# Unit vectors of the delta rule by whole tiles, and the paged attention's steps in other lanes

## The chip, the core and the metric

One core of one Trainium2 chip runs the whole program. The time is the device time of one execution in microseconds (us); less is better. The core has five engines with an instruction queue each: TensorE (PE) multiplies matrices into PSUM, VectorE (DVE) and ScalarE (ACT) work on vectors, GpSimd (POOL) on vectors too, and SyncE (SP) only starts transfers. GpSimd starts transfers as well. The engines run beside each other and meet only in semaphores: a waiting instruction holds everything behind it on its own engine.

## The reference

One decoder layer in float32 for a prompt of 512 tokens and a sample group of 8 sequences with 4 new tokens each, so T = 544 token columns in all. A mixer runs four head groups beside each other (block-sparse attention, Mamba-2 SSD, HGRN2, gated DeltaNet), then follow cross-attention and a SwiGLU network. Two parts matter here. The first is the unit vectors that the gated delta rule needs of its queries and keys, per token and head of 64 numbers:

```python
def l2_norm(x, eps=1e-6):
    return x * lax.rsqrt(jnp.sum(x * x, axis=-1, keepdims=True) + eps)
```

The query is also scaled by 1/8, and the kernel forms beta times k and beta times v beside it. The second is the sample group's attention over a paged cache of 16 pages per sequence: scores of all keys, the three best blocks of 256 tokens, a softmax, and the weighted sum of the values:

```python
    k_past = k_cache[layer, page_table].reshape(db, past, H, dh)
    gate = jnp.einsum('bqhd,bnhd->bhqn', q, kmean)
    _, idx = lax.top_k(gate, n_sel)
    p = jax.nn.softmax(sc.astype(jnp.float32), axis=-1)
```

## The kernel before

Activations lie with 128 features on the partitions and the 544 tokens in the free dimension, in two halves of 272 columns (`HT`), since a PSUM bank holds 512 floats. The program is a row of stages; each engine's part of a stage is a generator or function of its own, and a stage ends with a semaphore. The change lies in the stage called `ssm`. There four pieces of work are threaded by hand through each other on TensorE, VectorE and ScalarE alike. The string `LANES` holds one letter for each step: `m` is the main piece (`mixer_lane`), `p` the paged attention of the sample group (`moba_sample_*`), `u` the unit vectors of the delta rule (`unit_*`) and `n` a norm (`ssm_norm_*`). All three engines walk the same string and do their share of each step, so a step that must wait holds the steps behind it on that engine, whatever they belong to.

The main piece has 41 steps: the first is m0. m0 to m18 are the SSD scan over four prompt tiles and the sample tile (m16 is its sample tile, m17 its new sample states, m18 the gating). m19 to m26 are the eight levels of the HGRN2 attention on the prompt and m27 to m29 its three levels on the sample. In a level VectorE forms differences, ScalarE takes their exponential, VectorE multiplies queries and keys and then selects what TensorE has computed (L2309). m30 to m40 are the HGRN2 tail: m30 turns the first tile, and then each of the five tiles has two steps. m40 is the sample's second, and the last of the stage.

The paged attention has 111 steps. The first prepares the queries. Then j0 to j65 turn (transpose) the keys and score them: step j turns half a quarter and scores half j-2. A quarter is four pages, four transfers of 128 KB. Four idle steps follow, in the last of which VectorE ranks the blocks and ScalarE takes nine exponentials (L1553, L1554). T0 to T3 and one more step (called T4 here) turn the probabilities. Then come V0 to V31, one step for each quarter of the values, then a step in which VectorE normalizes, a step in which TensorE picks the heads apart (`pick`), and a last copy. There are four buffers for quarters. Quarter n is loaded by SP if n is even and by GpSimd if n is odd (`load_pages`), four pages each with a page number read from a table ahead of it. Value quarters of V4 and later wait until V(k-4) has been used.

The unit piece has 17 steps (`unit_tensor`, `unit_scalar`, `unit_vector`): ScalarE squares, TensorE sums the squares of each head onto 4 rows with `headsel` (64 ones per head), ScalarE takes Ln and Exp(-0.5 x) of the 4 rows, TensorE spreads each row over the 64 partitions of its head with `pairsel`, and VectorE multiplies out of PSUM, half by half. Six spreads are done: for two tiles of queries, two of keys, and two of beta. All of this uses the banks 5 and 6 and starts once the probabilities have been turned.

The list below writes the groups of steps between two main steps, where G k is what stands ahead of main step k.

```
G       before                                  after
0       queries, j0                             queries, j0
1-14    4, 3, 4, 3 ... of j (j1-49)             4 of j each (j1-56)
15, 16  j50-53; j54-56                          j57-59; j60-62
17, 18  j57-60; j61-63                          j63-65; idle
19, 20  j64 j65 idle; idle idle n               idle; idle n
21, 22  idle T0 n; T1 T2 n                      idle n; n
23, 24  T3 T4; V0 V1 u                          T0 T1; T2 T3
25      V2 V3 u                                 T4 V0
26-29   V4 V5 u; V6 V7 u; V8 V9 u; V10 V11 u    V1-3; V4-6; V7-9; V10-12
30      V12 V13 u                               V13-15
31-34   2 V and 2 u each (V14-21)               3 V and 1 u each (V16-27)
35, 36  V22 V23 2u; V24 V25                     V28 V29 u; V30 V31 u
37-39   V26 V27; V28 V29; V30 V31               u; u; u
40, 41  normalize, pick; copy                   normalize, pick; copy
```

Of the kernel before, what the change touches and what calls it, by code (L numbers as in the profile page):

```python
# [19 lines left out]
ALU = mybir.AluOpType  # L20
# [12 lines left out]
H = 4  # L33
# [34 lines left out]
def build(nc, a, o):  # L68
# [12 lines left out]
    with ctx:  # L81
# [298 lines left out]
        g_A = carve(PROJ, base + 2176, 2176)  # L380
        g_N = carve(PROJ, base + 2 * 2176, 2176)
        g_QK = carve(PROJ, base + 3 * 2176, 2176)
        g_sq = carve(XN, 2 * DH, 2, T)
        g_kb = carve(XN, 2 * DH, 2, T)
        g_norm = XN[0:H, 1216:1216 + T], SC[0:H, 8528:8528 + T]

        m = Carver(XN, 4 * T)
        t_tok = m(512)
# [995 lines left out]
        def moba_sample_tensor(pe):  # L1384
            def turn(j):

                n, c_ = divmod(j, 2)
                if c_ == 0:
                    pe.wait_ge(*pages_sem(n))
                if j >= 2:  # L1390
                    pe.wait_ge(S("keys_turned_s"), j - 1)
                for i in range(4):
                    last = tr(bank(5 + j % 2)[:, i * P:(i + 1) * P], pages[:, n % NPG, i, c_ * P:(c_ + 1) * P], P)
                last.then_inc(S("satt_turned"), 1)

            def score(j):

                n, c_ = divmod(j, 2)
                pg, e = divmod(n, 2)
                pe.wait_ge(S("keys_turned_s"), j + 1)  # L1400
                if j % 16 == 0:
                    pe.wait_ge(S("ms_scores_out"), j // 16 + 1)
                for g_ in range(4):
                    last = mm(bank(7)[32 * g_:32 * g_ + 32, pg % 4 * P:(pg % 4 + 1) * P], ms_qp[:, c_, 2 * g_ + e, :],
                              ms_kt[j % 2][:, g_ * P:(g_ + 1) * P], e == 0 and c_ == 0, e == 1 and c_ == 1)
                last.then_inc(S("satt_scored"), 1)

            pe.wait_ge(S("ms_q"), 1)
            for c_ in range(2):
                last = mm(bank(7)[:, 0:NS], ms_q[:, c_, :], ms_kown[:, c_, :], c_ == 0, c_ == 1)  # L1410
            last.then_inc(S("satt_rows"), 1)
            yield
            for j in range(66):
                if j >= 2:
                    score(j - 2)
                if j < 64:
                    turn(j)
                yield
            for _ in range(4):
                yield  # L1420
            pe.wait_ge(S("satt_exp"), 1)
            for i in range(4):
                if i >= 2:
                    pe.wait_ge(S("satt_pt_out"), i - 1)
                for k in range(4):
                    last = tr(bank(5 + i % 2)[:, k * P:(k + 1) * P], ms_s[:, (4 * i + k) * P:(4 * i + k + 1) * P], P)
                last.then_inc(S("satt_pt"), 1)
                yield
            pe.wait_ge(S("satt_pt_out"), 3)
            tr(bank(5)[0:NS, 0:P], ms_own, P).then_inc(S("satt_pt"), 1)  # L1430
            yield
            pe.wait_ge(S("satt_pt_out"), 5)
            for e in range(2):
                mm(bank(7)[:, e * GW:(e + 1) * GW], ms_pown[0:NS, :], ms_vown[0:NS, :], e == 0, False)
            for n in range(32, 64):
                pg, e = divmod(n - 32, 2)
                pe.wait_ge(*pages_sem(n))
                for g_ in range(4):
                    r = slice(32 * g_, 32 * g_ + 32)
                    last = mm(bank(7)[r, e * GW:(e + 1) * GW], st_all[:, pg, r], pages[:, n % NPG, g_, :], False, pg == NPAGE - 1)  # L1440
                last.then_inc(S("ms_values_used"), 1)
                yield
            yield
            pe.wait_ge(S("satt_o"), 1)
            pe.wait_ge(S("g_beta"), 6)
            pick = ident.rearrange("p (g e h t) -> p g e h t", e=2, h=H, t=TS)
            for e in range(2):
                for c_ in range(2):
                    for h2 in range(2):
                        last = mm(bank(5)[h2 * 64:h2 * 64 + 64, c_ * NS:(c_ + 1) * NS].rearrange("p (g e t) -> p g e t", e=2, t=TS)[:, :, e, :],  # L1450
                                  ms_o[:, e, (2 * c_ + h2) * DH:(2 * c_ + h2 + 1) * DH], pick[:, :, e, 2 * c_ + h2, :], True, True)
            last.then_inc(S("satt_pv"), 1)
            yield
            yield
# [196 lines left out]
        def half(ap, j):  # L1651
            return ap[:, j * HT:(j + 1) * HT]

        def spread_norm(pe, n):

            hp, kind = n % 2, n // 2
            src = rows[:, 2, :] if kind == 2 else g_norm[kind]
            for j in range(2):
                last = mm(bank(5 + j)[:, 0:HT], pairsel[0:H, hp, :], half(src, j), True, True)
            last.then_inc(S("rows_spread"), 1)  # L1660

        def unit_tensor(pe):
            yield
            for x in range(2):
                pe.wait_ge(S("satt_pt_out"), 5)
                pe.wait_ge(S("g_sq"), x + 1)
                if x:
                    pe.wait_ge(S("g_root"), 1)
                for hp in range(2):
                    for j in range(2):  # L1670
                        last = mm(bank(5 + j)[0:H, 0:HT], headsel[:, hp, :], half(g_sq[:, hp, :], j), hp == 0, hp == 1)
                last.then_inc(S("g_sum"), 1)
                yield
                yield
            pe.wait_ge(S("g_root"), 3)
            for n in range(6):
                if n:
                    pe.wait_ge(S("g_beta"), n)
                spread_norm(pe, n)
                yield  # L1680
                yield

        def unit_scalar(s):
            def squares(x):
                if x:
                    s.wait_ge(S("g_sum"), x)
                for hp in range(2):
                    last = A.activation(g_sq[:, hp, :], (gq, gk)[x][:, hp, :], ACT.Square)
                last.then_inc(S("g_sq"), 1)

            squares(0)
            yield
            yield
            for x in range(2):
                s.wait_ge(S("g_sum"), x + 1)
                for j in range(2):
                    last = A.activation(half(g_norm[x], j), two(5)[j][0:H, :], ACT.Ln, bias=eps[0:H, :])
                last.then_inc(S("g_root"), 1)
                if x == 0:
                    squares(1)  # L1700
                    yield
                    yield
            s.wait_ge(S("g_root"), 2)
            for x in range(2):
                last = A.activation(g_norm[x], g_norm[x], ACT.Exp, scale=-0.5)
            last.then_inc(S("g_root"), 1)
            yield
            for _ in range(12):
                yield

        def unit_vector(v):
            for _ in range(5):
                yield
            for n in range(6):
                yield
                hp, kind = n % 2, n // 2
                v.wait_ge(S("rows_spread"), 2 + n + 1)
                for j in range(2):
                    if kind == 0:
                        last = V.scalar_tensor_tensor(half(gq[:, hp, :], j), half(gq[:, hp, :], j), SCALE, two(5)[j], ALU.mult, ALU.mult)  # L1720
                    elif kind == 1:
                        last = tt(half(gk[:, hp, :], j), half(gk[:, hp, :], j), two(5)[j], ALU.mult)
                    else:
                        v.wait_ge(S("g_beta"), 4)
                        tt(half(g_kb[:, hp, :], j), half(gk[:, hp, :], j), two(5)[j], ALU.mult)
                        last = tt(half(gv[:, hp, :], j), half(gv[:, hp, :], j), two(5)[j], ALU.mult)
                last.then_inc(S("g_beta"), 1)
                yield


# [725 lines left out]
        def gdn_scalar(s):  # L2456
            hgrn_norm_scalar(s, 0)
            for i, (t0, w, _) in enumerate(TILES):
                s.wait_ge(S("g_m"), i + 1)
                ex = hl(g_p1[:, i % 4, :], w)  # L2460
                A.activation(ex, ex, ACT.Exp).then_inc(S("g_exp"), 1)
                if i < 4:
                    s.wait_ge(S("rows_spread"), 8 + i + 1)
                    A.activation(half(g_logd[:, i // 2, :], i % 2), bank(3 + 4 * (i % 2))[:, 0:HT], ACT.Copy).then_inc(S("rows_spread_out"), 1)
            s.wait_ge(S("rows_spread_out"), 4)
            link(A.activation(g_kbg, g_logd, ACT.Exp), "s")
# [408 lines left out]
        def mixer_lane(eng, ssm, hgrn):  # L2875
# [3 lines left out]
            yield from hgrn  # L2879


        LANES = "m".join(["pp"] + ["pppp", "ppp"] * 9 + ["ppp"] + ["ppn"] * 3 + ["pp"] + ["ppu"] * 7 + ["ppuu"] * 5
                         + ["pp"] * 5 + ["p"])

        def lanes(main, pages_, unit, norm):
            steps = {"m": main, "p": pages_, "u": unit, "n": norm}
# [148 lines left out]
```

## Time and profile before

| | |
|---|---|
| median of three runs | 1516.91 us (1513.17 to 1518.27) |
| the profiled execution's own time | 1517.02 us |
| its span in the trace | 1515.3 us |
| TensorE busy with matmuls | 1358.2 us, 90% |
| VectorE, ScalarE, GpSimd busy | 658.7, 467.9, 442.6 us |
| granted TensorE clock, mean | 0.907 of full speed |
| chain that ended last | TensorE 75%, VectorE 15%, ScalarE 4%, DMA 2% |

The stage runs from about 281 to 555 us of the span. A row of the timeline has the start, the length, the engine, the line, the operation, what it writes and reads, how many, and in brackets the idle time ahead of it with what ended it. L258 is the helper for matmuls, L261 the one for turning, L626 the one for VectorE's two-tensor operations. A float32 matmul or turn stands as two records. `W_scratch` holds the quarters. The clock column is 1.00 at 2.4 GHz and 0.50 at 1.2 GHz.

### The profile page before, as it was taken

The page shows a single profiled execution, that of the slowest core. Times are in us where ns is not written, and L with a number is a line of the kernel's source. Part 1 is how long each engine was busy: PE and PEld are TensorE (multiplying, and loading weights), DVE is VectorE, ACT ScalarE, POOL GpSimd, SP SyncE. Part 2 cuts the span into 40 slices and gives each one's busy share as a digit, 9 for nine tenths or more (in the row PEclk, how much of TensorE's full clock was granted, in tenths as well). Part 3 has the DMA queues.
Part 4 walks back from the last instruction along what each step waited for, and adds up shares of the span by engine and source line. Part 5 has one row for each costly group of instructions (what it writes and reads, how often), then busy time and mean ns, then how long its engine had stood idle before and what let it go on. Part 6 is the DMA issues. An engine that isn't in the chain of part 4 may idle for free.

```text
span 1515.3 us, 24848 instructions
## 1 busy us (share of the span) xinstructions
PE 1358.2 (90%) x10080; PEld 1184.4 (78%) x10080; DVE 658.7 (43%) x1104; ACT 467.9 (31%) x769; POOL 442.6 (29%) x370
## 2 busy tenths in 40 slices
PE   5997999889767976888989898989899999989999
PEld 4997987656554556787879784439899999989998
DVE  4569944254665236653242924310763333330003
ACT  3322244254233014123345423203532222222221
POOL 5424431323103402003525050003234433434330
PEclk8998999879757556998969999999999999999999
DMA  4222230346306630003333040451223223222321
GB/s 122 79 62 70 74 114 1 118 147 192 106 0 196 183 111 1 1 7 119 112 113 98 29 167 22 169 185 56 70 76 93 84 86 96 84 77 77 91 64 60
DMA packets 177556, 136.85 MB, mean 90 GB/s; under 512 B 15011, under 2 KB 165972, under 8 KB 177442
## 3 DMA queue, kind: packets, MB, share of 16 engines
q1 hardware_dynamic: 167906, 113.85, 24.8%
q0 software_dynamic: 7200, 20.23, 4.4%
q8 instruction: 80, 1.31, 0.4%
q10 hardware_dynamic: 2336, 1.18, 0.3%
q14 instruction: 34, 0.28, 0.1%
HBM read 127.27 MB, written 7.96 MB: 89 GB/s over the span
## 4 chain that ended last, share of the span: by engine, by line
PE 75%; DVE 15%; ACT 4%; issue 2%; DMA 2%; POOL 1%; SPq 1%; DVEq 0%; POOLq 0%; ACTq 0%
PE PS L258 69%; PE PS L261 6%; DVE PROJ L1746 2%; DVE SC L626 1%; DVE PROJ L626 1%; DVE XN L887 1%; DVE XT L626 1%; DVE XN L626 1%; POOL W_LO L242 1%; DMA W_scratch<-in_cache_moba_v 1%; DVE PROJ L1747 1%; DVE XN_parts L878 1%; DVE RSQ L885 0%; DVE OM L1595 0%; DMA PROJ<-in_x_sample 0%
## 5 line engine op out<-in xcount | busy, mean ns | idle before, releaser
L242 POOL TENSOR_TENSOR W_LO<-W,W_HI 128x1024 fp32r<-128x1024 f32 (+1 forms) x130 | 317.3, 2445 | 797.8 <-ACT W_HI L233 797.8
L258 PE MATMUL PS<-XN_parts,W_HI 128*128 128x272 f32 x1184 | 341.9, 289 | 0.0
L258 PE MATMUL PS<-OM_parts,W_HI 128*128 128x272 f32 x960 | 279.0, 291 | 0.0
L258 PE MATMUL PS<-SC_parts,W_HI 128*128 128x272 f32 (+2 forms) x832 | 246.7, 296 | 14.7 <-POOL W_LO L242 13.5
L258 PE MATMUL PS<-SC_parts,W_LO 128*128 128x272 f32 (+2 forms) x832 | 243.1, 292 | 0.0
L258 PEld LDWEIGHTS PS<-XN_parts,W_HI 128*128 128x128 f32 x1184 | 224.6, 190 | 0.0
L258 PE MATMUL PS<-OM_parts,W_LO 128*128 128x272 f32 x704 | 203.9, 290 | 0.0
L233 ACT ACTIVATE W_HI<-W 128x1024 fp32r<-128x1024 f32 (+1 forms) x130 | 134.1, 1041 | 207.5 <-PE PS L258 207.5
L258 PEld LDWEIGHTS PS<-OM_parts,W_HI 128*128 128x128 f32 x960 | 183.2, 191 | 0.1
L258 PEld LDWEIGHTS PS<-SC_parts,W_HI 128*128 128x128 f32 x832 | 159.3, 191 | 19.3 <-POOL W_LO L242 12.5
L258 PEld LDWEIGHTS PS<-SC_parts,W_LO 128*128 128x128 f32 x832 | 159.1, 191 | 0.0
L258 PE MATMUL PS<-PROJ_parts,W_HI 128*128 128x272 f32 (+2 forms) x608 | 153.1, 294 | 5.0 <-DVEq L2873 5.0
L258 PEld LDWEIGHTS PS<-OM_parts,W_LO 128*128 128x128 f32 x704 | 132.3, 188 | 0.0
L258 PEld LDWEIGHTS PS<-PROJ_parts,W_HI 128*128 128x128 f32 x608 | 109.1, 193 | 5.4 <-DVEq L2873 5.3
L258 PE MATMUL PS<-PROJ_parts,W_LO 128*128 128x272 f32 (+2 forms) x256 | 75.7, 296 | 0.0
L258 PE MATMUL PS<-SC,XN 64*64 64x4 f32 (+3 forms) x384 | 69.6, 327 | 0.0
L449 POOL DMA_DIRECT2D W_scratch<-in_cache_moba_v x64 | 34.3, 536 | 113.8 <-PE PS L258 83.4
L626 DVE TENSOR_TENSOR SC<-SC 128x272 f32<-128x272 f32 (+6 forms) x68 | 36.8, 544 | 70.5 <-ACT SC L820 50.9
L1147 ACT ACTIVATE PROJ<-PS 128x512 f32<-128x512 f32 (+1 forms) x76 | 44.9, 597 | 65.1 <-PE PS L261 52.8
L261 PE MATMUL PS<-CN,W_scratch 128*128 128x128 f32 x272 | 51.4, 319 | 14.1 <-ACT SC L1554 12.2
L258 PE MATMUL PS<-SC 64*128 64x128 f32 (+7 forms) x404 | 52.7, 345 | 11.7 <-DVE PROJ L626 5.2
L258 PE MATMUL PS<-PROJ,XN 128*128 128x128 f32 (+3 forms) x280 | 43.3, 306 | 20.1 <-DVE XN L626 19.6
(375 smaller groups left out, 2259.6 us busy)
## 6 DMA issues: line engine op xcount, KB each, us to landing
W<-in_w_gu SPq DMA_DIRECT2D x44, 512.0 KB, 3.7
W<-in_w_in SPq DMA_DIRECT2D x30, 512.0 KB, 3.6
W_scratch<-in_cache_moba_k SPq DMA_DIRECT2D x64, 128.0 KB, 2.7
W_scratch<-in_cache_moba_k POOLq DMA_DIRECT2D x64, 128.0 KB, 2.6
W_scratch<-in_cache_moba_v SPq DMA_DIRECT2D x64, 128.0 KB, 2.1
W_scratch<-in_cache_moba_v POOLq DMA_DIRECT2D x64, 128.0 KB, 2.8
W<-in_w_xkv SPq DMA_DIRECT2D x16, 512.0 KB, 3.5
W<-in_w_down SPq DMA_DIRECT2D x16, 512.0 KB, 3.6
```

Source lines behind the costliest of these rows:

```text
L233: nc.scalar.activation(hi_lo(n)[0], raw_chunk(n), ACT.Copy)\
L242: nc.gpsimd.tensor_tensor(hi_lo(n)[1], raw_chunk(n), hi_lo(n)[0].bitcast(F32), ALU.subtract).then_inc(S("weights_split"), 1)
L258: return nc.tensor.matmul(out, lhsT, rhs, start=start, stop=stop, skip_group_check=True)
L261: return nc.tensor.transpose(out, in_, ident[0:k, 0:k])
L449: eng.dma_start(pages[:, n % NPG, i, :], cache[0].rearrange("g p h d -> g p (h d)")[bass.ds(ids[i], 1)].rearrange("g p n -> (g p) n"))\
L626: return V.tensor_tensor(out, x, y, op)
L878: V.scalar_tensor_tensor(lo(k)[:, TOKENS[run][j]], XT[:, k, TOKENS[run][j]], par(GAINS[run][1] + k), hi(k)[:, TOKENS[run][j]].bitcast(F32) ...
L887: last = V.scalar_tensor_tensor(xn[:, k, c_], xn[:, k, c_], par(GAINS[run][0] + k), rsq[:, c_], ALU.mult, ALU.mult)
L1147: return A.activation(o_, i_, ACT.Copy)
L1746: V.scalar_tensor_tensor(dst[:, d:SEQ], src[:, 0:SEQ - d], wt[3 - d], dst[:, d:SEQ], ALU.mult, ALU.add)
L1747: last = V.scalar_tensor_tensor(ds_, win_[:, :, 3 - d:7 - d], wt[3 - d], ds_, ALU.mult, ALU.add)
```

## The change

The unit piece now works on one tile of 128 by 544 at a time, for four tiles (two of queries, two of keys): ScalarE squares the tile, TensorE multiplies the squares by `blk64`, a block matrix of ones, so that each partition gets the sum of its own head, ScalarE takes Ln out of PSUM and Exp(-0.5 x) over the whole tile, and VectorE multiplies from SBUF in one instruction. Only beta is still spread with `pairsel`. The piece has nine steps and three buffers of squares in place of two tiles of squares and two of norm rows. The string `LANES` is written anew, as in the list above. The counts in the waits of other stages follow.

```diff
-        g_sq = carve(XN, 2 * DH, 2, T)
+        g_sqs = [carve(XN, 2 * DH + i * T, T) for i in range(3)]
...
-            pe.wait_ge(S("g_beta"), 6)
+            pe.wait_ge(S("g_beta"), UNITS + 2)
...
         def unit_tensor(pe):
-            yield
-            for x in range(2):
-                pe.wait_ge(S("satt_pt_out"), 5)
-                pe.wait_ge(S("g_sq"), x + 1)
-                if x:
-                    pe.wait_ge(S("g_root"), 1)
-                for hp in range(2):
+            for x in range(UNIT_STEPS):
+                n = x - 1
+                if 0 <= n < UNITS:
+                    if n == 0:
+                        pe.wait_ge(S("satt_pt_out"), 5)
+                    else:
+                        pe.wait_ge(S("g_root"), 2 * n - 1)
+                    pe.wait_ge(S("g_sq"), n + 1)
                     for j in range(2):
-                        last = mm(bank(5 + j)[0:H, 0:HT], headsel[:, hp, :], half(g_sq[:, hp, :], j), hp == 0, hp == 1)
-                last.then_inc(S("g_sum"), 1)
+                        last = mm(bank(5 + j)[:, 0:HT], blk64, half(g_sqs[n % 3], j), True, True)
+                    last.then_inc(S("g_sum"), 1)
+                elif x in (5, 7):
...
+                    for j in range(2):
+                        last = mm(bank(5 + j)[:, 0:HT], pairsel[0:H, x // 7, :], half(rows[:, 2, :], j), True, True)
+                    last.then_inc(S("rows_spread"), 1)
                 yield
+
+        def unit_scalar(s):
+            for x in range(UNIT_STEPS):
+                n = x - 2
+                if 0 <= n < UNITS:
+                    s.wait_ge(S("g_sum"), n + 1)
+                    for j in range(2):
+                        last = A.activation(half(g_sqs[n % 3], j), two(5)[j], ACT.Ln, bias=eps)
+                    last.then_inc(S("g_root"), 1)
+                    s.wait_ge(S("g_root"), 2 * n + 1)
+                    A.activation(g_sqs[n % 3], g_sqs[n % 3], ACT.Exp, scale=-0.5).then_inc(S("g_root"), 1)
+                if x < UNITS:
+                    if x == 3:
+                        s.wait_ge(S("g_beta"), 1)
+                    A.activation(g_sqs[x % 3], unit_of(x), ACT.Square).then_inc(S("g_sq"), 1)
                 yield
...
         def unit_vector(v):
+            for x in range(UNIT_STEPS):
+                n = x - 2
+                if 0 <= n < UNITS:
+                    v.wait_ge(S("g_root"), 2 * n + 2)
+                    V.scalar_tensor_tensor(unit_of(n), unit_of(n), SCALE if n < 2 else 1.0, g_sqs[n % 3], ALU.mult, ALU.mult)\
+                        .then_inc(S("g_beta"), 1)
+                elif x in (6, 8):
+                    hp = x // 8
+                    v.wait_ge(S("rows_spread"), 2 + hp + 1)
+                    v.wait_ge(S("g_beta"), UNITS)
...
-        LANES = "m".join(["pp"] + ["pppp", "ppp"] * 9 + ["ppp"] + ["ppn"] * 3 + ["pp"] + ["ppu"] * 7 + ["ppuu"] * 5
-                         + ["pp"] * 5 + ["p"])
+        LANES = "m".join(["pp"] + ["pppp"] * 14 + ["ppp"] * 3 + ["p", "p", "pn", "pn", "n", "pp", "pp", "pp"] + ["ppp"] * 5
+                         + ["pppu"] * 4 + ["ppu", "ppu"] + ["u"] * 3 + ["pp", "p"])
```

## Rows read from the trace of the kernel before

**Rows 1.** The view by windows: engines' busy time, granted clock (PEclk), three stretches

```profile
core 0: us, PE busy (x) PEld busy (x) DVE busy (x) ACT busy (x) POOL busy (x), PEclk, DMA share, GB/s
460.00:470.00 10.00, 10.00 (x121) 7.13 (x114) 8.13 (x15) 5.56 (x7) 4.29 (x8) 1.00 0.52 170
...
510.00:520.00 10.00, 10.00 (x48) 4.85 (x44) 3.00 (x10) 0.00 (x0) 3.54 (x7) 0.50 0.44 125
...
560.00:580.00 20.00, 19.98 (x104) 16.15 (x102) 8.39 (x18) 6.11 (x10) 0.00 (x0) 0.50 0.25 82
```

**Rows 2.** Timeline of TensorE, key steps and the start of the levels

```profile
306.17 0.66 PE L258 MATMUL PS<-PROJ,W 128*32 128x128 f32 x8 [2.81 <-ACT PROJ L1147]
...
358.54 0.43 PE L258 MATMUL PS<-PROJ,W 128*32 128x128 f32 x8
...
359.49 0.43 PE L258 MATMUL PS<-PROJ,W 128*32 128x128 f32 x8
...
392.36 3.69 PE L258 MATMUL PS<-PROJ,SC 32*128 32x512 f32 x8
...
400.32 2.79 PE L258 MATMUL PS<-PROJ,W 64*128 64x128 f32 x32 [0.32 <-issue]
```

**Rows 3.** Timeline of VectorE: new sample states, ranking, and the first step after levels

```profile
396.17 2.48 DVE L626 TENSOR_TENSOR XN<-XN,PS 128x512 f32<-128x512 f32 x4 [5.42 <-PE PS L258]
...
419.75 0.46 DVE L626 TENSOR_TENSOR SC<-SC 128x64 f32<-128x64 f32 x2
...
481.54 0.35 DVE L2309 COPY_PREDICATED PROJ<-CN,PS 32x64 f32<-32x64 int32 x2 [5.35 <-PE PS L258]
```

**Rows 4.** Timeline of ScalarE: end of the exponentials, a table load, two squares

```profile
426.45 0.18 ACT L1554 ACTIVATION_READ_ACCUMULATOR SC<-SC 128x1 f32 x1
...
428.46 1.28 ACT L1981 ACT_TABLE_LOAD   x1
...
449.96 1.19 ACT L1688 ACTIVATE XN<-PROJ 128x544 f32<-128x544 f32 x2
```

**Rows 5.** Timeline of TensorE: probabilities, levels, and first value steps

```profile
426.69 1.12 PE L261 MATMUL PS<-CN,W_scratch 128*128 128x128 f32 x4 [12.15 <-ACT SC L1554]
...
453.15 1.94 PE L258 MATMUL PS<-W_scratch,PROJ 128*32 128x256 f32 x16
...
462.49 2.82 PE L258 MATMUL PS<-SC 64*128 64x128 f32 x32
```

**Rows 6.** Timeline of GpSimd: issues of the value quarters

```profile
455.77 1.71 POOL L449 DMA_DIRECT2D W_scratch<-in_cache_moba_v  x3 [53.94 <-PE PS L258]
...
471.55 2.30 POOL L449 DMA_DIRECT2D W_scratch<-in_cache_moba_v  x4 [2.27 <-issue]
476.11 2.30 POOL L449 DMA_DIRECT2D W_scratch<-in_cache_moba_v  x4 [2.26 <-issue]
```

**Rows 7.** Timeline of TensorE: value steps, unit steps and tail

```profile
477.12 1.93 PE L258 MATMUL PS<-W_scratch,PROJ 128*32 128x256 f32 x16 [3.61 <-DMA W_scratch<-in_cache_moba_v]
...
489.15 0.69 PE L261 MATMUL PS<-CN,SC 128*128 128x128 f32 x2 [5.66 <-DVE SC L626]
...
492.06 2.18 PE L258 MATMUL PS<-XN,CN 4*128 4x272 f32 x4
...
531.25 0.43 PE L258 MATMUL PS<-SC,XN 64*64 64x128 f32 x2
...
535.16 1.08 PE L258 MATMUL PS<-W_scratch,PROJ 128*32 128x256 f32 x8 [1.15 <-DMA W_scratch<-in_cache_moba_v]
537.64 1.04 PE L258 MATMUL PS<-CN,W 128*64 128x16 f32 x16 [1.40 <-DVE W L1526]
```

**Rows 8.** Timeline of VectorE: a unit step, the masked values of the sample, the stage's end

```profile
499.29 0.79 DVE L626 TENSOR_TENSOR PROJ<-PROJ,PS 128x272 f32<-128x272 f32 x2 [3.56 <-PE PS L258]
...
533.02 2.49 DVE L626 TENSOR_TENSOR SC<-XN,CN 32x512 f32<-32x512 f32 x4
...
550.97 1.23 DVE L626 TENSOR_TENSOR XN<-XN,SM 128x1024 f32<-128x1024 f32 x1 [3.46 <-PE PS L258]
```

More of the change, by code:

```diff
@@ L382, in build @@
         g_QK = carve(PROJ, base + 3 * 2176, 2176)
-        g_sq = carve(XN, 2 * DH, 2, T)
+        g_sqs = [carve(XN, 2 * DH + i * T, T) for i in range(3)]
         g_kb = carve(XN, 2 * DH, 2, T)
-        g_norm = XN[0:H, 1216:1216 + T], SC[0:H, 8528:8528 + T]
         m = Carver(XN, 4 * T)
@@ L1652, in half @@
             return ap[:, j * HT:(j + 1) * HT]
[L1654 to L1660, printed above, removed]
-        def unit_tensor(pe):
-            yield
-            for x in range(2):
-                pe.wait_ge(S("satt_pt_out"), 5)
-                pe.wait_ge(S("g_sq"), x + 1)
-                if x:
-                    pe.wait_ge(S("g_root"), 1)
-                for hp in range(2):
-                    for j in range(2):
-                        last = mm(bank(5 + j)[0:H, 0:HT], headsel[:, hp, :], half(g_sq[:, hp, :], j), hp == 0, hp == 1)
-                last.then_inc(S("g_sum"), 1)
[L1673 to L1680, printed above, removed]
+        UNITS = 4
@@ new lines, in build, with unit_of @@
+        UNIT_STEPS = 9
+        def unit_of(n):
+            return (gq, gk)[n // 2][:, n % 2, :]
+        def unit_tensor(pe):
+            for x in range(UNIT_STEPS):
[6 more added lines that the diff above has]
+                    pe.wait_ge(S("g_sq"), n + 1)
+                    for j in range(2):
+                        last = mm(bank(5 + j)[:, 0:HT], blk64, half(g_sqs[n % 3], j), True, True)
+                    last.then_inc(S("g_sum"), 1)
+                elif x in (5, 7):
+                    if x == 5:
+                        pe.wait_ge(S("g_root"), 2 * UNITS - 1)
+                    else:
+                        pe.wait_ge(S("g_beta"), UNITS + 1)
+                    for j in range(2):
+                        last = mm(bank(5 + j)[:, 0:HT], pairsel[0:H, x // 7, :], half(rows[:, 2, :], j), True, True)
+                    last.then_inc(S("rows_spread"), 1)
@@ L1681, in unit_tensor @@
                 yield
         def unit_scalar(s):
[L1684 to L1708, printed above, removed]
+            for x in range(UNIT_STEPS):
[11 more added lines that the diff above has]
+                    A.activation(g_sqs[x % 3], unit_of(x), ACT.Square).then_inc(S("g_sq"), 1)
@@ L1709, in unit_scalar @@
                 yield
         def unit_vector(v):
[L1712 to L1724, printed above, removed]
+            for x in range(UNIT_STEPS):
[8 more added lines that the diff above has]
+                    v.wait_ge(S("g_beta"), UNITS)
+                    for j in range(2):
@@ L1725, in unit_vector @@
                         tt(half(g_kb[:, hp, :], j), half(gk[:, hp, :], j), two(5)[j], ALU.mult)
                         last = tt(half(gv[:, hp, :], j), half(gv[:, hp, :], j), two(5)[j], ALU.mult)
-                last.then_inc(S("g_beta"), 1)
+                    last.then_inc(S("g_beta"), 1)
                 yield
@@ L2462, in gdn_scalar @@
                 if i < 4:
-                    s.wait_ge(S("rows_spread"), 8 + i + 1)
+                    s.wait_ge(S("rows_spread"), 4 + i + 1)
                     A.activation(half(g_logd[:, i // 2, :], i % 2), bank(3 + 4 * (i % 2))[:, 0:HT], ACT.Copy).then_inc(S("rows_spread_out"), 1)
```

## The prediction

> **What bounds the kernel now.** Read the page first: TensorE is busy for 90% of the span and carries 75% of the chain that ended last, so TensorE's waits and its clock are what can change. The change touches one stage, 281 to 555 us, so the next view is TensorE's timeline there. It shows three regimes.
>
> In the key steps TensorE is nearly always busy. At the upper clock one j step starts 0.95 us after another (358.54, 359.49) [rows 2]; the few gaps follow ScalarE's exponentials of the SSD scan, such as 2.81 us at 306.17 [rows 2], and after that gap the same score step takes 0.66 us in place of 0.43 for a while.
>
> In the eight levels (400 to 470 us) VectorE and ScalarE alternate, and TensorE has time to spare. Its longest wait is 12.15 us ahead of 426.69, for the last exponential of the paged softmax, because T0 stands in front of level 2 in G21 [rows 5]. It looks like the prize of this change, but is not: ScalarE itself does those exponentials until 426.63, and level 2's own exponential stands behind them on ScalarE in both kernels [rows 4].
>
> From 489 to 531.7 us (tail and values) TensorE is busy throughout. Its granted clock is 0.50, that is 1.2 GHz, in 510 to 520 though it is busy for 10.00 of 10 us, while 460 to 470 with the same 10.00 had 1.00 [rows 1]. Beside it runs a second bound: GpSimd issues four transfers of a value quarter in 2.30 us, and then spends 2.26 us on "issue", the page numbers of the next one, so it starts one quarter every 4.56 us (471.55, 476.11) [rows 6]. As it brings every second quarter, the values can't go faster than 2.28 us each. TensorE has met this bound once as a real wait, 3.61 us at 477.12 [rows 7].
>
> **1. Key steps at four a lane.** The number of steps is unchanged, only five more of them stand ahead of m17 (66 against 61). At 0.95 us, less the last two, which only score, that is 4.2 us. Against it, steps moved up fill the gaps behind exponentials: one step more fits ahead of each early exponential, and where the gap shrinks, the slow clock may not follow it. From the 2.81 us gap and its like I take 3 us back; bounds 0 and 8. m17's matmuls (392.36) [rows 2] come 1.2 us later, and so do VectorE's additions at 396.17 that close the sample states [rows 3]. Level 0 can't start before these end. Before, j61 to j65 hid that wait (the row at 400.32 has no wait but 0.32) [rows 2]; now TensorE stands idle for about 2.5 us there. That costs nothing by itself, since VectorE leads the levels, but their start goes 1.2 us later.
>
> **2. Softmax and levels.** VectorE's chain from 396.17 to the ranking at 419.75 [rows 3] has the same instructions in the same order, so it is 1.2 us late. Moving T0 behind m22 takes its copy out of ScalarE's queue: the table load at 428.46 can start at the end of the exponentials, 426.63, so 1.8 us are won [rows 4]. T0 to T4 now stand in G23 to G25, where TensorE has slack. Net: the levels are 0.6 us earlier from G22 on, and their period by VectorE is what it was. The won 12.15 us of TensorE turn into other idle time.
>
> **3. Values start later.** Before, V0 and V1 run at 453.15 (two in 1.94 us, 0.97 each at the low clock) [rows 5], so V1 ends at 455.1, and GpSimd starts the next quarter at 455.77 [rows 6]. Now V1 stands behind level 6 (m25), whose matmuls are at 462.49 and last 2.82 us at the upper clock, twice that at the lower [rows 5]. V1 ends at 465.5 to 469; I take X = 467, 12 us later. What of V2 to V13 ran in the shadow of the levels must now run after them, and the page numbers pace it: V5 can be used at X + 6.3 (issue 0.7 after V1, four transfers in 2.6, then about 3 to land, as 473.85 to 477.12 for V11), and V(5+2k) at X + 6.3 + 4.56 k [rows 6, 7]. V11 is at X + 20. Level 2 of the sample (m29) stands behind V12, so at X + 22; its result and the tail's preparation take VectorE and ScalarE 7.6 us (481.54 to 489.15, less 0.8 for a unit step that stands between) [rows 3, 7]. So m30 turns its first tile at X + 29 to 30, after V15 (X + 29.1 and its own 1): 497 against 489.15, **+7.9 us**.
>
> **4. Tail with values and units.** Before, m30 to m38 take from 489.15 to 531.68, 42.5 us, with 16 value steps and five unit steps of TensorE among them [rows 7]. Now the same main steps hold V16 to V31, 16 again, and six unit steps: four block sums and two spreads. Both are two float32 matmuls of 128 partitions by 272 columns, as the row at 492.06, 2.18 us (its weights are 4 rows high, and the row of a 128-row pair elsewhere is no longer, the columns being the same) [rows 7]. One more is **+2.2 us**. The two dropped head sums stood among the levels, where they were hidden: 0. Page waits: V17, V19 and V21 are due at X + 33.7, 38.2, 42.8 while TensorE, at 2.28 us of pages a value against 0.97 of its own, has only 1.2 to 1.8 us of main work between groups of three. I count 5 us of waits until V21, and none after, when units and main steps cover it: **+5 us**, bounds 2 and 8. The clock: before, this stretch was at the low level but for its last part (the row at 531.25 is 0.43 for two matmuls) [rows 7]; I take the same. Check from the other side: V31 can't land before X + 6.3 + 13 times 4.56 = X + 65.6 = 532.6, and m36, m37, m38 and two spreads still stand behind it, 10 us at the upper clock and 17 at the lower, so m38 ends at 543.6 to 551. The sum above gives 531.7 + 15.1 = 546.8, within that.
>
> **5. Units on ScalarE and VectorE.** ScalarE loads a table for Ln and one for Exp in each of four steps, 1.28 us each, with about four passes of 0.6: some 5 us a step, ten of 20 us in all being table loads [rows 4]. ScalarE does nothing else in the tail. A lane there lasts about 9 us, so neither VectorE, which waits for it, nor the main step queued behind VectorE's wait is late: 0; if a lane were under 6 us, it would cost 1 us each. VectorE's last unit step (four products, twice 0.79) now stands directly ahead of m39, whose masked values (2.49 us) and the normalization lead to `pick`: **+1.5 us** [rows 8].
>
> **6. The end.** From the end of m38 at 531.68 to VectorE's first instruction after m40 at 550.97 are 19.3 us [rows 7, 8]. Ahead of V31 at 535.16, TensorE waited for its page; that about 0.9 us is gone, as V31 is done long before: **-0.9 us**.
>
> The sum is 7.9 + 2.2 + 5 + 1.5 - 0.9 = 15.7 us later at the end of the stage; everything behind it moves along. Against the profiled execution's own 1517.02 us (0.1 above the median) that is 1532.7, and I say 1532.5.
>
> **Rivals.** (a) *TensorE gets the upper clock in the tail.* For it: 531.25 shows that it comes back there [rows 7]. Against it: the page waits leave new gaps, and 510 to 520 was busy without one and stayed low [rows 1]. Then only pages bound the tail: V31 at 532.6, 10 us of TensorE, 19.3 - 0.9 + 1.5 of end, less 5 if m40 too is fast: 557.5 to 562.5, +7 to +11; I say 1526. The Trainium skill's page "TensorE: Matmul & The Clock Gate" (Part 1, The HAM clock gate) says that the gate follows how busy the array has recently been and opens after a short busy stretch; by that rule this rival would be the rule and not the exception. The row of 510 to 520 speaks against it, so it keeps a small chance.
>
> (b) *The low clock holds all through*, also in levels and the end of the tail: X is 469, m38 takes the 17 us. m38 at X + 6.3 + 59.3 + 17 + some 3 of blocked value steps = 554.6, and the end +23 to +26: 1542.
>
> (c) *The key steps win what I hold for lost:* all early gaps and slow stretches close, 8 instead of 3 us. Then X is 462 and all behind it 5 us earlier: 1527.5, with (a) 1520, no change that can be told.
>
> (d) *Faster, by the clock at the stage's end.* If TensorE arrives at m40 at the upper level and keeps it into the next stage, where 560 to 580 are 19.98 us busy at 0.50 [rows 1], up to 10 us are won there and 5 in m40. With (a)'s +7 that already counts m40, the time is 1514 or less. [...]
>
> (e) *The change does nothing:* not open here, since V1 stands behind level 6 by the order of the steps.
>
> **How the numbers follow.** Forecast (1526.5 to 1538) 0.48; (a) 0.13; (b) 0.14; (c) 0.12, a third of it within 0.3% of before; (d) 0.10; something that takes back about all, 0.03. About 0.3%, 4.5 us, is what can be told from no change. Faster: (d) and a tenth of what takes back all, 0.10. Same: the rest of that 0.03, 0.04 of (c) and the low edge of (a), 0.03: 0.10. Slower: 0.80. The range leaves (d) out below and the worst of (b) above: 1517 to 1543.
>
> **What would show it.** After the change, V1 should end at 465 to 469; GpSimd should issue at a strict 4.56 us from there to V15 and past it, and TensorE's waits in G27 to G33 should be put down to pages of the values; the wait of 12.15 us should be gone and the ranking within 3 us of 419.75; m30 at about 497; `pick` waiting some 5 to 7 us for VectorE; the stage's end near 566. It is wrong if the ranking comes more than 5 us earlier, if value steps come faster than one in 2.28 us for long, or if 490 to 550 shows a clock near 1.00.

## The result, and the profile after

| | before | after |
|---|---|---|
| median | 1515.04 us (4 runs, 1512.83 to 1518.27) | 1542.72 us (4 runs, 1541.14 to 1543.84) |
| ratio to before | | 1.018, 95% interval 1.0156 to 1.0204 |
| profiled execution, its span | 1517.02, 1515.3 us | 1541.14, 1539.2 us |
| TensorE busy in the span | 1358.2 us | 1353.8 us |

The change costs 1.8%, 27.7 us between the medians and 24.1 us between the two profiled executions. TensorE does 4.4 us less work and waits for more. The first view is the chain that ended last, from the page of the changed kernel: TensorE has lost share to issue and ScalarE, and the page numbers (L439 on GpSimd's queue) are on it.

```profile
PE 72%; DVE 16%; ACT 5%; issue 4%; DMA 1%; POOLq 1%; POOL 1%; SPq 0%; DVEq 0%; ACTq 0%
PE PS L258 66%; PE PS L261 6%; DVE PROJ L1733 2%; DVE SC L626 1%; DVE PROJ L626 1%; POOLq L439 1%; DVE XN L626 1%; DVE XN L887 1%; DVE XT L626 1%; POOL W_LO L242 1%; DVE PROJ L1734 1%; DVE XN_parts L878 1%; DVE PROJ L2296 1%; DVE RSQ L885 0%; DVE OM L1595 0%
```

TensorE's timeline of the changed kernel, at the steps that answer to [rows 2, 5, 7]: first key page, m16, the two key steps that only score, m17, levels 0, 2 and 3, T0 T1, V0, level 6, V1 to V3, V7 V8, m30, V21, a unit step at the upper clock, two more waits in the tail, the last outputs of m38, and `pick`.

```profile
284.30 1.12 PE L261 MATMUL PS<-CN,W_scratch 128*128 128x128 f32 x4 [2.87 <-DMA W_scratch<-in_cache_moba_k]
...
382.20 6.73 PE L258 MATMUL PS<-SC 32*64 32x32 f32 x72
...
392.06 1.41 PE L258 MATMUL PS<-PROJ,W 128*32 128x128 f32 x16
393.40 7.19 PE L258 MATMUL PS<-PROJ,SC 32*128 32x512 f32 x8
403.33 5.10 PE L258 MATMUL PS<-PROJ,W 64*128 64x128 f32 x32 [2.73 <-DVE XN L626]
...
422.71 5.10 PE L258 MATMUL PS<-SC 64*128 64x128 f32 x32 [2.03 <-DVE PROJ L2296]
437.57 5.10 PE L258 MATMUL PS<-SC 64*128 64x128 f32 x32 [9.76 <-DVE PROJ L2296]
442.60 1.97 PE L261 MATMUL PS<-CN,W_scratch 128*128 128x128 f32 x8
...
460.26 1.08 PE L258 MATMUL PS<-W_scratch,PROJ 128*32 128x256 f32 x8
461.28 5.13 PE L258 MATMUL PS<-SC 64*128 64x128 f32 x32
466.34 1.75 PE L258 MATMUL PS<-W_scratch,PROJ 128*32 128x256 f32 x24
...
478.40 1.94 PE L258 MATMUL PS<-W_scratch,PROJ 128*32 128x256 f32 x16 [1.63 <-DMA W_scratch<-in_cache_moba_v]
...
497.30 0.69 PE L261 MATMUL PS<-CN,SC 128*128 128x128 f32 x2
...
510.03 1.08 PE L258 MATMUL PS<-W_scratch,PROJ 128*32 128x256 f32 x8 [3.51 <-DMA W_scratch<-in_cache_moba_v]
...
516.07 1.18 PE L258 MATMUL PS<-XN,CN 128*128 128x272 f32 x4
...
521.25 1.73 PE L258 MATMUL PS<-W_scratch,PROJ 128*32 128x256 f32 x16 [3.56 <-DMA W_scratch<-in_cache_moba_v]
526.69 1.08 PE L258 MATMUL PS<-W_scratch,PROJ 128*32 128x256 f32 x8 [3.71 <-DMA W_scratch<-in_cache_moba_v]
...
549.34 0.69 PE L258 MATMUL PS<-SC,XN 64*64 64x128 f32 x2
556.82 1.04 PE L258 MATMUL PS<-CN,W 128*64 128x16 f32 x16 [6.79 <-DVE W L1526]
```

The wait of 12.15 us for the softmax [rows 5] is gone, and in its place level 3 waits 9.76 us for VectorE. Two rows of VectorE in the changed kernel mark the ranking and the end of the stage.

```profile
424.28 0.46 DVE L626 TENSOR_TENSOR SC<-SC 128x64 f32<-128x64 f32 x2
...
570.14 1.22 DVE L626 TENSOR_TENSOR XN<-XN,SM 128x1024 f32<-128x1024 f32 x1 [3.46 <-PE PS L258]
```

Where the time came from is read by marks, each counted from the first turned key page (before at 286.37, after at 284.30), since the part ahead of the stage differed by 2 us between the two traces. The ranking is the mark that the row at 424.28 answers to, m38 ends with the last of its outputs (549.34, 0.69 long), and the end of the stage is the row at 570.14. Two rows of the kernel before, its first turned key page and its m16:

```profile
286.37 1.11 PE L261 MATMUL PS<-CN,W_scratch 128*128 128x128 f32 x4 [1.94 <-DMA W_scratch<-in_cache_moba_k]
...
379.81 5.63 PE L258 MATMUL PS<-SC 32*64 32x32 f32 x72
```

| mark | before | after | later by |
|---|---|---|---|
| m17 starts | 106.0 | 109.1 | 3.1 |
| ranking | 133.4 | 140.0 | 6.6 |
| m30 | 202.8 | 213.0 | 10.2 |
| end of m38 | 245.3 | 265.7 | 20.4 |
| end of the stage | 264.6 | 285.8 | 21.2 |

The waits summed by releaser, 440 to 560 us, say which resource: of the changed kernel TensorE waited 11 times for value pages, and GpSimd had 14 gaps that nothing but its own page numbers filled. In the kernel before these were 3 waits of 6.5 us in all and 7 gaps of 12.8.

```profile
POOL W_scratch L449 <- issue: 28.8, 14, 2.8
PE PS L258 <- DMA W_scratch<-in_cache_moba_v: 27.8, 11, 3.7
```

The windows 430 to 490 and 490 to 550, before and after (columns as in [rows 1]):

```profile
430.00:490.00 60.00, 47.41 (x369) 34.87 (x368) 38.58 (x67) 21.88 (x33) 15.02 (x28) 0.64 0.39 124
490.00:550.00 60.00, 55.76 (x366) 30.83 (x364) 16.27 (x44) 0.00 (x0) 15.75 (x29) 0.59 0.47 133
```

```profile
430.00:490.00 60.00, 37.23 (x309) 27.10 (x309) 33.60 (x59) 12.58 (x22) 10.74 (x20) 0.61 0.31 94
490.00:550.00 60.00, 40.27 (x284) 19.67 (x284) 14.42 (x32) 20.81 (x30) 20.07 (x37) 0.70 0.54 162
```

In the levels TensorE is busy for 10.2 us less, and in the tail it is idle for 19.7 of 60 us although much is left to do.

### The profile page after: what moved, and what is told of

It is laid out like the page before. It is cut to its first block, busy times and chain, and to the rows that moved or that the text cites. A ratio compares the mean times of both kernels' runs of the same rounds, so it can differ in the third digit from the quotient of the medians.

```text
span 1539.2 us, 24821 instructions
## 1 busy us (share of the span) xinstructions
PE 1353.8 (88%) x10064; PEld 1180.0 (77%) x10064; DVE 658.0 (43%) x1100; ACT 476.5 (31%) x779; POOL 442.9 (29%) x370
## 3 DMA queue, kind: packets, MB, share of 16 engines
q10 hardware_dynamic: 2336, 1.18, 0.3%
## 4 chain that ended last, share of the span: by engine, by line
PE 72%; DVE 16%; ACT 5%; issue 4%; DMA 1%; POOLq 1%; POOL 1%; SPq 0%; DVEq 0%; ACTq 0%
PE PS L258 66%; PE PS L261 6%; DVE PROJ L1733 2%; DVE SC L626 1%; DVE PROJ L626 1%; POOLq L439 1%; DVE XN L626 1%; DVE XN L887 1%; DVE XT L626 1%; POOL W_LO L242 1%; DVE PROJ L1734 1%; DVE XN_parts L878 1%; DVE PROJ L2296 1%; DVE RSQ L885 0%; DVE OM L1595 0%
## 5 line engine op out<-in xcount | busy, mean ns | idle before, releaser
L258 PE MATMUL PS<-SC 64*128 64x128 f32 (+7 forms) x404 | 52.8, 343 | 23.9 <-DVE PROJ L2296 16.3
L258 PEld LDWEIGHTS PS<-SC 64*128 64x128 f32 (+5 forms) x404 | 43.5, 227 | 33.2 <-DVE SC L626 22.2
```

What stands on the lines that cost most here:

```text
L258: return nc.tensor.matmul(out, lhsT, rhs, start=start, stop=stop, skip_group_check=True)
```

## The experiments

Each kernel was timed in turn with the kernel before on its chip; the ratio is to those runs. "Stage" is the time from the first turned key page to the mark 570.14 answers to, in the kernel's own trace: 264.6 us before, 285.8 after.

### The two halves of the change: e1 and e2

e1 has the new unit vectors, with the paged steps where they were and the units in G29 to G37.

```diff
+        LANES = "m".join(["pp"] + ["pppp", "ppp"] * 9 + ["ppp"] + ["ppn"] * 3 + ["pp"] * 6 + ["ppu"] * 9 + ["pp"] * 3 + ["p"])
```

> The whole-tile unit vectors alone. The paged steps stand as before (T0 ahead of level 2, V0 V1 in G24), the nine unit steps in G29 to G37. Theory (the loss comes from where the paged steps stand): the new units cost one more TensorE step in the tail at 1.1 to 2.2 us and one VectorE step ahead of pick, so the time is that of before within 4 us (1511 to 1519). Rival (the new units themselves are slow, by table loads and full-height block sums): 1525 or more.

Measured: 1512.57 us, ratio 0.9987 (0.9966 to 1.0009), stage 259.3. No difference that can be told. In the profiled execution the stage is 5.3 us shorter than before, and all of that is there by m30, which stands 197.2 us after the first key page in place of 202.8. Ahead of m30, G24 to G28 hold no unit steps any more.

e2 has the old unit vectors with the new places of the paged steps.

```diff
+        LANES = "m".join(["pp"] + ["pppp"] * 14 + ["ppp"] * 3 + ["p", "p", "pn", "pn", "n", "pp", "pp", "pp"]
+                         + ["pppu"] * 5 + ["pppuu"] * 4 + ["ppuu"] * 2 + [""] * 3 + ["pp", "p"])
```

> The old unit vectors with the paged steps placed as in the changed kernel; the seventeen unit steps fill G26 to G36. Theory: the placing carries the loss, 1535 to 1545, and V1 ends near 467. Rival (units): as before, 1512 to 1520.

Measured: 1539.49 us, ratio 1.0171 (1.0144 to 1.0199), stage 289.1. The placing carries the loss. The new arithmetic is neutral by the medians; by the stage, e1 against before and the changed kernel against e2, it saves 5.3 and 3.3 us. e1 moves the unit steps as well, and one trace each does not settle a difference of that size.

### ScalarE's table loads: e7

```diff
-                        last = A.activation(half(g_sqs[n % 3], j), two(5)[j], ACT.Ln, bias=eps)
+                        last = A.activation(half(g_sqs[n % 3], j), two(5)[j], ACT.Exp, scale=-0.0001)
...
-                    A.activation(g_sqs[n % 3], g_sqs[n % 3], ACT.Exp, scale=-0.5).then_inc(S("g_root"), 1)
+                    A.activation(g_sqs[n % 3], g_sqs[n % 3], ACT.Exp, scale=-4.0).then_inc(S("g_root"), 1)
```

> The changed kernel with Exp of a tiny scale in place of Ln in the unit steps and another scale in the second Exp, so its unit vectors have wrong lengths; the number and shapes of instructions stay, but the eight table loads between Ln and Exp go. Theory: ScalarE has slack in the tail, so the time is that of the changed kernel within 2 us. Rival (VectorE and then TensorE wait for ScalarE's loads): 4 to 8 us faster.

Measured: 1540.34 us, ratio 1.015 (1.0116 to 1.0183), stage 285.6 against 285.8. From 490 to 570 us ScalarE loads 8 tables in the changed kernel and none in e7, so the loads are free in the tail. The medians, 2.4 us apart, can't tell this from the rival's 4 us; the stage does. That the rest of the 5 us that a unit step takes on ScalarE is free as well isn't tested by this run.

### The spacing of the key steps: e5

```diff
+        LANES = "m".join(["pp"] + ["pppp", "ppp"] * 9 + ["ppp", "ppn", "pn", "n", "pp", "pp", "pp"] + ["ppp"] * 5
+                         + ["pppu"] * 4 + ["ppu", "ppu"] + ["u"] * 3 + ["pp", "p"])
```

> The changed kernel with the key steps up to G18 spaced as before (four and three in turn) and j64, j65 in G19; everything from T0 on stands as changed. Theory: m17's matmuls run at the upper clock again (3.7 us and not 7.2), the ranking comes 5 to 6.6 us earlier after the stage's start, and the whole is 4 to 7 us faster than the changed kernel. Rival (the later start of the levels is absorbed in the page-paced part): the ranking is earlier, but the end is within 2 us of the changed kernel.

Measured: 1531.35 us, ratio 1.0106 (1.007 to 1.0141), stage 281.0. In the stage that is 4.8 us of the changed kernel's 21.2 recovered, within the 4 to 7 that I expected. The medians stand 11.4 us apart, which is more; 5.7 us of the difference between the two profiled executions lies outside the stage, and no run says why. Its TensorE timeline shows m17, and level 0, which follow without a wait behind the key steps:

```profile
389.79 3.69 PE L258 MATMUL PS<-PROJ,SC 32*128 32x512 f32 x8
...
397.71 2.79 PE L258 MATMUL PS<-PROJ,W 64*128 64x128 f32 x32 [0.29 <-issue]
```

The same m17 took 7.19 us in the changed kernel, and in e2, e3 and e7, which share its spacing. It took 3.7 to 4.5 us in all eight traces with the old one. The ranking comes at 133.1 after the first key page, against 140.0, and m30 at 206.0, against 213.0; of these 7 us 4.8 are left at the end of the stage. m17 follows m16, small matmuls of 32 by 32, within which the granted clock falls to 0.50 in both kernels. Before, four full key steps stood between the two, 5.4 us long (386.94 to 392.36), and near 391, 4 us into them, the clock returned to 1.00. Now three do, of which two only score: 3.0 us (390.43 to 393.40), all at 0.50, and so are m17's large matmuls and level 0 behind them (5.10 us in place of 2.79).

### The page numbers: e3, e4 and e10

e3 is the changed kernel and e4 the kernel before, both with constant page numbers for the values, so that other pages are read.

```diff
-                ids = [eng.value_load(PTAB[0:1, (2 * i + e) * NPAGE + pg:(2 * i + e) * NPAGE + pg + 1], min_val=0,
-                                      max_val=a["cache_moba_k"].shape[1] - 1) for i in range(4)]
+                ids = [(4 * n + i) % 128 for i in range(4)] if n >= 32 else \
+                      [eng.value_load(PTAB[0:1, (2 * i + e) * NPAGE + pg:(2 * i + e) * NPAGE + pg + 1], min_val=0,
+                                      max_val=a["cache_moba_k"].shape[1] - 1) for i in range(4)]
...
```

> The changed kernel with constant page numbers for the value quarters, so the values that it reads are other ones; the number and size of transfers are the same. It takes the 2.26 us of page numbers from each of GpSimd's value quarters. Theory: the values were paced at 4.56 us per GpSimd quarter; now at 2.3, the 15 us of page waits in G27 to G35 fall to under 3 us, and the time falls by 8 to 15 us, to 1528 to 1535; the rest of the loss (later start, main steps behind V31) stays. Rival (transfers themselves or TensorE's low clock bound the tail): less than 3 us.

Measured: 1531.27 us, ratio 1.0104 (1.0071 to 1.0136), stage 275.1, so 10.7 us shorter. TensorE's waits for value pages from 455 us on fall from 27.8 to 16.6 us, not to near nothing as expected. The pace is no longer GpSimd's: it now issues four transfers in 2.12 us and waits for TensorE, with four buffers between them. Transfers also land later: the median of GpSimd's is 3.5 us after the issue, against 3.0 in the changed kernel.

```profile
491.07 2.12 POOL L450 DMA_DIRECT2D W_scratch<-in_cache_moba_v  x4 [1.06 <-PE PS L258]
495.20 2.12 POOL L450 DMA_DIRECT2D W_scratch<-in_cache_moba_v  x4 [2.01 <-PE PS L258]
```

> The kernel before with constant page numbers for the value quarters (other values are read). Its values start 12 us earlier and wait for pages only 3.6 us at 477 and 2.3 us at 533. Theory: it gains 1 to 4 us only, so the page pace costs it little; the difference to the changed kernel shrinks to about 14 us. Rival (page pace bounds both alike): it gains as much as the changed kernel does.

Measured: 1506.04 us, ratio 0.9955 (0.9918 to 0.9992), stage 251.9. The kernel before gains as well, against my theory, and the two stay 23 us apart by the stage where I expected 14. Its waits for value pages from 455 us on did not fall (6.7 us, 6.5 before). What changed is the clock: its tail ran at the upper level from 493 us on. Was that chance? e9 is the kernel before, unchanged, for a second trace, and e10 is e4 again.

> The kernel before, unchanged, for a second trace. What is asked is whether TensorE's low clock from 489 to 524 us is fixed for this order of work. If fixed: m30 to m38 take 42 to 43 us again, and the time outside the stage is 1250.7 us within 0.5. If it varies from one execution to the next: 30 to 45 us, and up to 5 us of difference outside the stage.

Measured: 1516.62 us, ratio 1.0007 (0.9984 to 1.0031), stage 264.7, m30 to m38 42.5 us as in the first trace. The slow tail of the kernel before is its own. The time outside the stage came out at 1253.2 us, and not within 0.5 of 1250.7 as I had expected of a fixed order.

> The kernel before with constant page numbers for the value quarters, once more (other values are read). In its first trace TensorE had the upper clock from 493 us on and the tail was 12 us shorter. If that came with the faster pages: again upper clock by 495 us and a stage 10 to 13 us shorter. If it was chance: a tail near 42 us, and a stage within 3 us of before.

Measured: 1505.68 us, ratio 0.9946 (0.992 to 0.9973), stage 257.3. So the gain is real, 8 us by the medians of both, though the clock ran differently: 1.00 again at 494 to 499, but 0.50 from 504 to 514. The same 5 us of the kernel before, of e4 and of e10, and then 504 to 509 of e10 (columns as in [rows 1]):

```profile
494.00:499.00 5.00, 5.00 (x25) 2.48 (x24) 1.45 (x4) 0.00 (x0) 2.14 (x4) 0.50 0.74 209
494.00:499.00 5.00, 4.39 (x55) 2.24 (x54) 2.44 (x8) 0.00 (x0) 2.88 (x6) 1.00 0.92 267
494.00:499.00 5.00, 3.95 (x48) 2.12 (x48) 2.63 (x8) 0.00 (x0) 3.18 (x7) 1.00 0.97 309
504.00:509.00 5.00, 5.00 (x26) 2.50 (x26) 0.42 (x1) 0.00 (x0) 1.75 (x4) 0.50 0.45 131
```

Page numbers cost both kernels time, the changed one by waits (11.2 us fewer in e3) and the one before by the clock. What the page pace explains is a part of the changed tail's idle time, not the difference between the kernels. Why the kernel before, whose TensorE was busy all through, gets more of the upper clock when GpSimd and SP have less to do is not settled. e4 and e10 also read other pages than the kernel before, and no run separates the two.

### Values earlier: e6, and the end: e8

e6 takes the changed unit vectors and the old key spacing, and puts T0 to T4 and V0, V1 between levels 2 and 3, where TensorE waits for VectorE in the changed kernel. The values then go in pairs and not in threes, and the units stand two groups earlier, in G29 to G37.

```diff
+        LANES = "m".join(["pp"] + ["pppp", "ppp"] * 9 + ["ppp", "ppn", "pn", "pppppppn"] + ["pp"] * 6 + ["ppu"] * 9
+                         + ["", "", "pp", "p"])
```

> New units, key steps as before, but T0 to T4 and V0, V1 all in G22, between levels 2 and 3, V2 to V13 in pairs in G23 to G28, V14 to V31 in pairs with the units in G29 to G37. Theory (the start of the values sets how long page pace matters, and T0's copy ahead of level 2's exponential costs 1.8 us): V1 ends near 442, no page wait in the tail, 1 to 6 us faster than the kernel before. Rival (TensorE at its low clock bounds levels and tail, whatever the pages do): within 2 us of the kernel before, or slower by up to 4.

Measured: 1509.78 us, ratio 0.9964 (0.9941 to 0.9988), stage 256.8. Against e5, which differs only from T0 on, the stage is 24.1 us shorter. No run separates what the early start, the pairs and the place of the units each bring. TensorE's timeline: by the marks V0 starts 26 us and V1 ends 31 us earlier than in the changed kernel. Page waits of 12.6 us remain in the tail and ahead of it, where I expected none in the tail.

```profile
433.58 1.94 PE L258 MATMUL PS<-W_scratch,PROJ 128*32 128x256 f32 x16
...
476.69 2.21 PE L258 MATMUL PS<-W_scratch,PROJ 128*32 128x256 f32 x16 [2.53 <-DMA W_scratch<-in_cache_moba_v]
...
498.62 1.08 PE L258 MATMUL PS<-W_scratch,PROJ 128*32 128x256 f32 x8 [4.42 <-DMA W_scratch<-in_cache_moba_v]
...
527.24 1.04 PE L258 MATMUL PS<-CN,W 128*64 128x16 f32 x16 [5.40 <-DVE W L1526]
```

The last row is the next bound: `pick` waits for a normalization that stands behind m39's masked values on VectorE. e8 moves both ahead; the edit is shown against e6.

```diff
-                         + ["", "", "pp", "p"])
+                         + ["p", "p", "", "p"])
```

> The early-values kernel with the normalization in G38 and pick in G39, ahead of m39 and m40, in place of G40. Theory: pick no longer waits 5 to 7 us for VectorE behind m38 (masked values, last unit step, normalization); m40's outputs start once the tokens are copied, and the masked values are made beside them. The stage is 3 to 5 us shorter than with early values alone, and 8 to 10 us faster than the kernel before. Rival (m40 waits for VectorE's copies anyway and its last matmuls for the masked values): under 1.5 us.

Measured: 1503.15 us, ratio 0.9929 (0.9904 to 0.9955), stage 250.5, 6.3 us shorter than e6, more than the 3 to 5 expected. 5.8 us of it lie between the end of m38 and the end of the stage, 12.9 us in place of 18.7. It is the fastest kernel of the case, 0.7% below before. `pick` no longer waits, and m40 starts 0.88 us behind it:

```profile
524.11 0.65 PE L258 MATMUL PS<-CN,W 128*64 128x16 f32 x16
525.63 0.27 PE L258 MATMUL PS<-PROJ,XN 32*64 32x32 f32 x2 [0.88 <-DVE XN L2149]
```

## Why the prediction was right in direction and short in size

The forecast was 1532.5 us with a range of 1517 to 1543; 1542.72 lies in the range, at its upper edge, beside rival (b) at 1542. Rival (b) held a low clock all through; the clock column shows 0.70 in 490 to 550, more and not less than before. That the range holds at all, by 0.3 us, owes something to luck: two of its terms were wrong in opposite directions, as follows.

**Key steps, step 1: forecast 1.2 us, measured 6.6 at the ranking.** This is the step that failed, and with it the sign that the ranking would come within 3 us of 419.75: it came at 424.28. m17 starts 3.1 us late instead of 1.2, and its matmuls take 7.19 us in place of the 3.69 that I carried over [rows 2]. My sum for the five steps was itself half a microsecond too high: with two that only score, at 0.43 us a row [rows 2], it is 3.7 and not 4.2. The 3 us that I took back were too many: six more steps, 5.7 us, stand ahead of m16, which starts 4.5 us later, so only 1.2 came back. m16 itself takes 1.1 us more (6.73 against 5.63), and the shorter group behind it gives 2.4 back. I had priced what the new spacing might win back from the clock, and not what it might lose; e5 shows that the spacing is the cause. The time lost passes to VectorE's additions and then unchanged to the ranking. Behind it not all of it lasts.

**Softmax, step 2: right to a tenth.** From the ranking to level 2's selections are 12.4 us in place of 14.2 (436.70 in the changed kernel, 433.97 before): the 1.8 us that T0's copy took on ScalarE. TensorE's wait of 12.15 us was no prize: it went to 9.76 us of waiting elsewhere.

**Start of the values, step 3: the numbers met, by two errors that cancel.** V1 was to end at 465.5 to 469 and ends at about 467; m30 was to come at 497, and comes at 497.30. With a ranking 5.4 us later than forecast both should have come some 5 us later. What made it up are the levels, whose period I had held to be VectorE's alone: from level 4 to level 6 the changed kernel takes 12.5 us (448.82 to 461.28), the one before 16.4 (446.12 to 462.49). Before, V0 to V3 and a unit step of TensorE stood there, now only V0, and levels 5 and 6 began without a wait behind them, so that work was only partly hidden. e5 shows the same from the other side: without the loss in the key steps, m30 is 3.2 us late and not 6.7 (7.9 less 1.2). From V1 on the pace is the one forecast, 30.4 us to m30 in place of 29 to 30. Levels 4 and 5 of the kernel before, then level 4 of the changed one:

```profile
446.12 5.10 PE L258 MATMUL PS<-SC 64*128 64x128 f32 x32 [3.22 <-DVE PROJ L2309]
...
455.02 4.73 PE L258 MATMUL PS<-SC 64*128 64x128 f32 x32
```

```profile
448.82 4.84 PE L258 MATMUL PS<-SC 64*128 64x128 f32 x32 [4.26 <-DVE PROJ L2296]
```

GpSimd's issues of the changed kernel hold 4.56 us over most of the stretch:

```profile
472.77 2.29 POOL L449 DMA_DIRECT2D W_scratch<-in_cache_moba_v  x4 [2.26 <-issue]
477.33 2.29 POOL L449 DMA_DIRECT2D W_scratch<-in_cache_moba_v  x4 [2.27 <-PE PS L258]
481.89 2.30 POOL L449 DMA_DIRECT2D W_scratch<-in_cache_moba_v  x4 [2.27 <-issue]
```

The stage also started 2.1 us earlier than before, so m30 is 10.2 us late by the marks, not 7.9.

**Tail, step 4: forecast 7.2 us, measured 10.2 (52.7 against 42.5).** The extra unit step is there. The page waits were mis-sized: I counted 5 us up to V21 and none after. They are 13.8 us between m30 and m38: V17, V19 and V21 wait 6.5 us (3.51 of it at 510.03), and V25 and V27, of which I expected nothing, 7.3 (3.56, 3.71). By my reading, which no run isolates, main steps that get the upper clock are too short to cover three quarters at 2.28 us. The clock paid some of it back: four of the six unit steps took 1.18 or 1.19 us and not 2.18, and the outputs of m36 0.43 us a pair. In all TensorE is busy for 37.4 us there, 5.2 less than before, and waits 15.4 more. The other mistake is what the pace was held for. e4 and e10 show that slow page numbers cost the kernel before about as much, so the difference between the kernels is TensorE's work moved out of the levels, where most of it was hidden, into the tail: 10.2 us of busy time less in 430 to 490. The 24.1 us between e5 and e6 say the same, with the pairs and the units' places changed beside it.

**Units, step 5: right.** ScalarE's table loads cost nothing (e7), and the new unit steps as a whole cost nothing that the times can tell (e1). **End, step 6:** 20.1 us against 19.3, forecast +0.6; `pick` waits 6.79 us, forecast 5 to 7.

**Beyond the stage.** By the marks the stage accounts for 21.2 us. I took it that the rest only moves along. In the twelve traces of this study, none of which changes anything outside the stage, span less stage lies between 1246.7 us (e10) and 1255.6 (e7); it is 1250.7 before, 1253.4 after. Two traces of one kernel lie 2.6 us apart there (before and e9) and 5.7 (e4 and e10). So the 2.7 us of the profiled 23.9 that lie outside are within that scatter. Whether the 6.5 us that the medians show beyond the stage are scatter too isn't shown; one trace of the changed kernel can't say.

## What to carry to other kernels

A long wait of the busiest engine is worth removing only if what stands behind it was late: look at what the engine that feeds the next step does in that time, here ScalarE with the same exponentials in both orders. Work that has a long supply line (32 quarters at a fixed cost of issue each) should start as early as its first input allows, in the shadow of whatever bounds that stretch. In e5, where V1 ends 7 us later than before, it and the work around it cost 16.4 us of the stage. Where steps of several pieces share one order on every engine, look at the last few for waits behind another piece's work: moving two steps ahead of two others won 6.3 us of the stage (e8).

## What the runs showed of the hardware

- TensorE's clock at one place can hang on a few small steps ahead of it. Eight m17 matmul records took 7.19 us in the four traces with the new spacing, behind 3.0 us of key steps, and 3.7 to 4.5 us in the eight with the old, behind 5.4 to 6.1 us of them. In both of the traces that the timelines above show, TensorE was busy for all but 0.1 us of these steps.
- Busy time alone did not fix the clock. The kernel before kept 0.50 from 489 to 524 us in both of its traces, and TensorE was busy for 41.85 and 41.36 of the 42 us from 489 to 531; with constant page numbers the same TensorE instructions had 1.00 from about 493 us in one trace (e4), and from 491 to 499 in the other (e10). The Trainium skill's page "TensorE: Matmul & The Clock Gate" (Part 1, The HAM clock gate) ties the clock to recent activity and lets it rise once the engine is busy. The kernel before doesn't bear this out for 35 us of busy TensorE, and why is open.
- Four transfers that take their pages from a table cost GpSimd 2.26 us for the page numbers beside 2.30 us for the issues. With constants the four issues alone take 2.12 us.
- The span outside the stage, the same code in all twelve traces, scatters by 9 us, while the stage of the kernel before came out at 264.6 and 264.7 us. That is not so of every kernel: with constant page numbers (e4, e10) it was 251.9 and 257.3, as the clock ran differently. Marks inside a stage can tell apart what medians of a few runs can't, but a difference of 5 us wants a second trace, which e1, e5 and e8 did not get.
